# Differential attention: the second score pass widened to 128 rows, transposes kept in one PSUM bank and interleaved with the value product

## The reference, cut to what matters

```python
def diff_attention(q, k, v, lam):
    def attend(qb):
        s = jnp.einsum('bqhcd,bkhcd->bhcqk', qb, k).astype(jnp.float32) * scale
        p = jax.nn.softmax(s, axis=-1)
        a = p[:, :, 0] - lam_f * p[:, :, 1]
        o = jnp.einsum('bhqk,bkhd->bqhd', a, vf)
```

## Time and profile before

| | |
|---|---|
| median of 3 runs | 3091.17 us |
| profiled execution: device time | 3091.63 us |
| its span, first to last instruction | 3089.9 us |
| mean granted TensorE clock | 0.944 |
| TensorE matmul busy | 2802.0 us (91%) |
| VectorE / ScalarE / GpSimd busy | 1243.7 / 945.5 / 464.8 us |
| attention of layer 0, first score matmul to last copy of o | 2010.1 to 2234.1 us |
| attention of layer 1, first score matmul to last value product | 2764.0 to 2965.5 us |

### The profile page before, as it was taken

The page is one execution under the profiler, slowest core; times in us unless marked ns, Lnnn a source line. Parts: engine busy times, 40 slices in busy tenths (PEclk is TensorE's granted clock), DMA queues, the critical chain, the costliest instruction groups (busy, mean ns, idle before and its releaser), DMA issues. The chain is left out here.

```text
span 3089.9 us, 35833 instructions
## 1 busy us (share of the span) xinstructions
PE 2802.0 (91%) x14783; PEld 2349.1 (76%) x14783; DVE 1243.7 (40%) x1549; ACT 945.5 (31%) x1482; POOL 464.8 (15%) x277
## 2 busy tenths in 40 slices
PE   4999677999979999999947999999987999989989
PEld 1877565898768888888837999777777998767767
DVE  4742752434353333333365222255544412226652
ACT  3312332444141122111122212256522222135640
POOL 0100121332000000000001000066510000007630
PEclk9999889999989999999978999989988999989989
DMA  5531001001111111111112132221022113232112
GB/s 212 177 123 47 14 8 49 13 1 69 41 41 48 48 48 48 48 48 48 48 56 78 45 76 59 72 52 47 1 83 96 57 51 70 52 79 49 42 69 82
DMA packets 63598, 184.97 MB, mean 60 GB/s; under 512 B 7392, under 2 KB 26208, under 8 KB 61792
## 3 DMA queue, kind: packets, MB, share of 16 engines
q1 hardware_dynamic: 63456, 182.96, 18.8%
HBM read 148.93 MB, written 16.97 MB: 54 GB/s over the span
## 5 line engine op out<-in xcount | busy, mean ns | idle before, releaser
L1543 DVE TENSOR_REDUCE da_negmax<-ps 128x1 f32<-128x1040 f32 x136 | 168.8, 1241 | 118.6 <-PE ps L1421 93.6
L2030 DVE SCALAR_TENSOR_TENSOR res<-ps,gates,res 128x1024 f32<-128x1024 f32 x64 | 79.2, 1280 | 226.1 <-PE ps L2079 226.1
L1452 PE MATMUL ps<-da_aT,v 128*128 128x128 f32 (+1 forms) x1224 | 165.7, 281 | 2.5 <-DVE da_aT L1479 2.3
L1452 PEld LDWEIGHTS ps<-da_aT,v 128*128 128x128 f32 x1224 | 151.5, 196 | 19.8 <-issue 15.6
L1529 POOL TENSOR_TENSOR da_E<-da_E,da_F 128x1040 f32<-128x1040 f32 x68 | 163.3, 2401 | 5.7
L2079 PE MATMUL ps<-ff_h_lo,ff_wh 128*128 128x512 f32 x512 | 157.8, 389 | 0.0
L2079 PE MATMUL ps<-ff_h_hi,ff_wh 128*128 128x512 f32 x512 | 157.8, 389 | 0.0
L2079 PE MATMUL ps<-ff_h_hi,ff_wl 128*128 128x512 f32 x512 | 157.6, 389 | 0.0
L1993 ACT ACTIVATE ff_wh<-ff_raw 128x1024 fp32r<-128x1024 f32 x64 | 67.5, 1057 | 284.2 <-PE ps L2079 278.4
L1527 POOL TENSOR_SCALAR da_F<-da_F,da_mixed 128x1040 f32<-128x1040 f32 x68 | 77.4, 1138 | 498.9 <-DVE da_mixed L1554 497.5
L2067 PE MATMUL ps<-ffn_in_hi,ff_wh 128*128 128x512 f32 x480 | 148.8, 391 | 2.2 <-DVE ff_wl L2016 2.2
(11 more groups left out here) (426 smaller groups left out, 6308.1 us busy)
## 6 DMA issues: line engine op xcount, KB each, us to landing
ff_raw<-w_ff SPq DMA_DIRECT2D x64, 512.0 KB, 3.3
ada_w<-w_ada SPq DMA_DIRECT2D x16, 1024.0 KB, 7.3
wo_ring<-w_out SPq DMA_DIRECT2D x18, 512.0 KB, 4.8
residual_spill<-res SPq DMA_DIRECT2D x2, 4160.0 KB, 11.2
st_q<-st_q_rounded SPq DMA_DIRECT2D x32, 260.0 KB, 5.1
res<-xT SPq DMA_DIRECT2D x2, 4096.0 KB, 14.4
ada_w<-w_ada SPq DMA_DIRECT2D x4, 2048.0 KB, 26.6
pqk_raw<-w_in SPq DMA_DIRECT2D x16, 512.0 KB, 4.4
```

What stands on the lines that cost most here:

```text
L1452: mm = pe.matmul(k.ps[:, 7, 0:w], v(g // NQ, t), aT[g % 2][:, t, 0:w], start=(t == 0), stop=(t == NT - 1))
L1543: dve.tensor_reduce(nm[:, n % 4:n % 4 + 1], window(n), AX.X, ALU.max, negate=True).then_inc(s_nm, 1)
L2030: last = dve.scalar_tensor_tensor(out=res[:, m, :], in0=k.ps[:, 4 * s + 2 * t:4 * s + 2 * t + 2, :].rearrange("p c w -> p (c w)"), scalar= ...
```

## The change

It does four things.

1. The second score pass has 128 rows: stationary [q low; q low], moving the whole [k high; k low]. For this `copy` gains three DMAs of 64 x 1040 elements. Two write component 1's q low to both halves of a second tile (the slot that held the k low part); they wait for the eight earlier DMAs. The third writes component 0's q low over the other half of its own tile, and waits for those two. PIECES is 11, and `wait_built` waits for all eleven.
2. All transposes use bank 6, and bank 7 holds the value product alone. turn(i,1) now waits for the copy of batch 0, turn(i,2) for the copy of batch 1, and pv(i,0) for out(i-1).
3. On TensorE turn(i,0) moves ahead of pv(i-1,1), so that the value product stands between batches 0 and 1. On ScalarE out(i-1) moves ahead of exps(g,0) of the next iteration.
4. ScalarE's `round` moves from groups 0 and 1 of a head to groups 3 and 4, and GpSimd's `rest` from ahead of groups 1 and 2 to ahead of groups 4 and 5.

```diff
-    bank = (6, 7, 6)
+    bank = 6
...
                     elif b == 1:
-                        if g:
-                            pe.wait_ge(s_o, g)
+                        pe.wait_ge(s_at, 2 * g + 1)
                     else:
-                        pe.wait_ge(s_at, 2 * g + 1)
+                        pe.wait_ge(s_at1, g + 1)
...
                     if part == 0:
-                        pe.wait_ge(s_at1, g + 1)
-                        pe.wait_ge(s_at, 2 * g + 1)
+                        if g:
+                            pe.wait_ge(s_o, g)
...
                     if g < NG:
                         scores(g, 0)
+                    if 0 <= i < NG:
+                        turn(i, 0)
                     if i >= 1:
                         pv(i - 1, 1)
                     if 0 <= i < NG:
-                        turn(i, 0)
                         turn(i, 1)
...
-                for g in range(NG + LAG):
+                for g in range(NG + LAG + 1):
                     i = g - LAG
-                    if i >= 0:
+                    if 0 <= i < NG:
                         evacuate(act, i, 0, s_at)
+                    if i >= 1:
+                        out(i - 1)
                     if g < NG:
                         exps(g, 0)
-                        if g // NQ + 1 < heads and g % NQ < 2:
-                            stacks.round(act, g // NQ + 1, g % NQ)
+                        if g // NQ + 1 < heads and 3 <= g % NQ <= 4:
+                            stacks.round(act, g // NQ + 1, g % NQ - 3)
...
-                    if i >= 0:
-                        out(i)
...
-                    if g // NQ + 1 < heads and 1 <= g % NQ <= 2:
-                        stacks.rest(pool, g // NQ + 1, g % NQ - 1)
+                    if g // NQ + 1 < heads and 4 <= g % NQ <= 5:
+                        stacks.rest(pool, g // NQ + 1, g % NQ - 4)
...
-    PIECES = 8
+    PIECES = 11
...
         sp.wait_ge(self.s_low, done + 2)
+        sp.wait_ge(self.s_built, 16 * (before + 8))
+        for r in range(2):
+            sp.dma_start(low[half[r], :].bitcast(F32), qlow[half[1], :].bitcast(F32)).then_inc(self.s_built, 16)
+        sp.wait_ge(self.s_built, 16 * (before + 10))
+        sp.dma_start(qlow[half[1], :].bitcast(F32), qlow[half[0], :].bitcast(F32)).then_inc(self.s_built, 16)
...
-        half = slice(64 * c, 64 * c + 64)
         kk = self.k[h % 2][c]
-        return [(self.q[h % 2][c][:, qa:qa + w], kk), (self.low[half, h, qa:qa + w], kk[half, :])]
+        return [(self.q[h % 2][c][:, qa:qa + w], kk), (self.low[:, AH * c + h, qa:qa + w], kk)]
```

More of the change, by code:

```diff
@@ L1432, in turn @@
                     elif b == 1:
-                        if g:
-                            pe.wait_ge(s_o, g)
+                        pe.wait_ge(s_at, 2 * g + 1)
                     else:
-                        pe.wait_ge(s_at, 2 * g + 1)
+                        pe.wait_ge(s_at1, g + 1)
                     for j, t in enumerate(batch[b]):
-                        tr = pe.transpose(k.ps[:, bank[b], j * P:(j + 1) * P], E[g % 4][:, t * P:(t + 1) * P], k.ident[:])
+                        tr = pe.transpose(k.ps[:, bank, j * P:(j + 1) * P], E[g % 4][:, t * P:(t + 1) * P], k.ident[:])
                     tr.then_inc(s_T, 1)
@@ L1477, in evacuate @@
                 dst = aT[g % 2][:, 4 * b:4 * b + nb, 0:w]
-                src = k.ps[:, bank[b], 0:nb * P].rearrange("p (t q) -> p t q", t=nb)[:, :, 0:w]
+                src = k.ps[:, bank, 0:nb * P].rearrange("p (t q) -> p t q", t=nb)[:, :, 0:w]
                 (eng.activation(dst, src, ACT.Copy) if sem is s_at else eng.tensor_copy(dst, src)).then_inc(sem, 1)
@@ L1635, in copy @@
                 sp.dma_start(q[c][half[r], 0:L2].bitcast(F32), self.qh[half[c], :].bitcast(F32)).then_inc(self.s_built, 16)
+        qlow, before = self.low[:, h, :], self.PIECES * (h - self.head)
         sp.wait_ge(self.s_low, done + 2)
+        sp.wait_ge(self.s_built, 16 * (before + 8))
[3 more added lines that the diff above has]
+        sp.dma_start(qlow[half[1], :].bitcast(F32), qlow[half[0], :].bitcast(F32)).then_inc(self.s_built, 16)
     def wait_built(self, pe, h):
@@ L1640, in wait_built @@
             pe.wait_ge(self.s_built, 16 * self.PIECES * (h - self.head + 1))
-            pe.wait_ge(self.s_low, 2 * (h - self.head + 1))
     def passes(self, h, c, qa, w):
-        half = slice(64 * c, 64 * c + 64)
         kk = self.k[h % 2][c]
-        return [(self.q[h % 2][c][:, qa:qa + w], kk), (self.low[half, h, qa:qa + w], kk[half, :])]
+        return [(self.q[h % 2][c][:, qa:qa + w], kk), (self.low[:, AH * c + h, qa:qa + w], kk)]
 def latent_heads(nc, k, name, heads, NQ, splits, n_keys, v, scale, o_dst, e0, at0, then, then_at):
```

## The result

| | before | after |
|---|---|---|
| median, us | 3089.57 (4 runs, 3087.89 to 3092.67) | 3060.86 (4 runs, 3050.50 to 3066.28) |
| profiled execution, us | 3091.63 | 3063.95 |
| its span, us | 3089.9 | 3062.2 |
| mean granted clock | 0.944 | 0.946 |
| attention of layer 0, us | 223.8 | 196.8 |

The ratio of the times is 0.9898, with a 95% interval of 0.9874 to 0.9922: the change makes the kernel about 1.0% faster. The forecast was 3072, with a range of 3050 to 3090. The two attention rows count from the first score matmul to the last value product.

A forecast was written before the change was run, and what follows sets the result against it. TensorE was taken to set the pace. Iterations -52.1, phase ends -1.9 and -1.0, phase starts +5.0, head waits +17.9 and +3.5, clock +9.0 sum to -19.6 us from 3091.63: forecast 3072, range 3050 to 3090.

The forecast's parts named there:

- the likeliest case: Whole kernel: the forecast's own sum of terms holds and the time is 3072 us; given 60 in 100.
- the forecast's own signs of being wrong: Attention: iteration above 5.4 us, a head's first scores without a gap, or turn 1 or 2 waiting in every iteration.
- The iteration, 4.95 us: TensorE's steady attention iteration falls from 5.79 to 4.95 us; over 62 iterations -52.1 us.
- Rival 1: Score passes: gaps at pass ends stay whatever the row count; iteration 5.66 us, time 3105; one in ten.
- The waits in 4.90: Turns 1 and 2: new waits for ScalarE and VectorE fit a 4.90 us iteration by 0.06 and 0.02; 0.05 added.
- Phase starts, +5.0: Start of each attention phase: the three added DMAs delay the scores by 2.3 us in layer 0, 2.7 in layer 1.
- The chain at the heads: Later heads: late round, rest and DMAs end 25.7 us after the fifth group's start, TensorE waiting 5.9 us in layer 1.
- 17.9: Three later heads of layer 1: TensorE stands 5.9 us at each, waiting for the DMA chain, +17.9 us.
- gaps of 3.5: Later heads of layer 0: TensorE stands 1.1 to 1.2 us at each, +3.5 us.
- The clock, +9.0: Behind the three head gaps of layer 1: half clock costs 3.0 us each, +9.0 us.
- lead-in and drain as forecast: Phase ends: three iterations ahead per phase save 0.31 us each (-1.9), six at the end some 0.17 each (-1.0).
- the forecast's 0.2%, 6 us: Whole kernel: the smallest difference in time that a measurement can tell from no change, 0.2% or 6 us.

The follow-up runs named there:

- e2: The change with the second score pass back on 64 rows, without the three added DMAs: 3073.9 us, ratio 0.9936.
- e3: The kernel before with only the second score pass on 128 rows (eleven DMAs), old order, banks and places: 3060.68 us, ratio 0.9886.
- e4: The change with the norm's product on VectorE taking one tensor and two per-partition scalars instead of two tensors: 3059.12 us, ratio 0.9889.
- e5: The change with round and rest back at the head's start and the norm's product on one tensor: 3041.29 us, ratio 0.9825.
- e6: e5 with the q low copies waiting only for the four k DMAs, not all eight: 3037.66 us, ratio 0.9809.
- e7: The change with pv(i-1,1) ahead of turn(i,0) again on TensorE, all transposes still in one bank: 3099.61 us, ratio 1.0010.
- e1: The change with only the move of round and rest undone, back at the start of the head: 3047.65 us, ratio 0.9843.
- e8: The change with the q low copies waiting only for the four k DMAs, not all eight: 3051.75 us, ratio 0.9860.

## Why the prediction was right

The time came out 11 us below the 3072 forecast, inside the range, and the likeliest case happened. But two of the forecast's own signs of being wrong came in part: the first scores of the three later heads of layer 0 follow without a gap, where 1.1 us was put, and turn 2 waits in every iteration, for 0.15 us. Point by point:

1. *The iteration, 4.95 us.* Measured 4.96, scores 1.04 for 1.03. e2 and e3 show that the row count does most of it: 0.61 us under the new order, 0.75 under the old. Rival 1 is refuted. The Trainium skill's rule (TensorE: Matmul & The Clock Gate, Part 3, The mechanism), that weight loads overlap only where row groups differ, does not hold here as it stands; in e2 they stand idle for 0.25 us where the row count changes, and with the change on 128 rows throughout no such idle time is listed. (The same section also lets a load run ahead into a background weight buffer; no run here shows which buffer is used.) The forecast also read more into the rule than it says: the 64 rows of a narrow pass lie among the 128 of its neighbours, and its three loads use the same rows, so the rule gives the narrow pass no overlap either. And the earlier trace rows, on which it rested, show matmuls only, no loads.
2. *The waits in 4.90.* Turn 1 fits. Turn 2 waits 0.15 in the weight load, where 0.02 were left and 0.05 had been added.
3. *Phase starts, +5.0.* The gaps grew from 2.96 and 2.95 to 5.17 and 4.88: 2.2 for 2.3, and 1.9 for 2.7.
4. *The chain at the heads.* Forecast from the fifth group: +9.0, +18.2, +22.6, +25.7; measured +9.01, +18.03, +22.26, +25.14. TensorE was to be there at +19.8 and came at +21.93. Of these 2.1 us, 1.9 are VectorE's hold-up. **This is the step that failed**: "The head's remaining groups give TensorE 4 x 4.95" took every iteration as undisturbed, although `rest` runs in two of them. In layer 1 the error hides itself: gaps of 9.6 and hold-ups of 5.6 sum to 15.3, for 17.9. In layer 0 the hold-up alone is there, 5.6 us, for gaps of 3.5. In all 20.9 us stand against 21.4 forecast. In layer 1 the two causes had to balance, since a later TensorE waits less; that they nearly do in layer 0 is luck. (The 17.9 is also 3 x 5.9 = 17.7, rounded up.)
5. *The clock, +9.0.* Measured 5.1 behind the gaps: the term was mis-sized, since it was taken from a gap of 5.83 and the gaps were 3.2, of which one was followed by no fall at all. In e4, with gaps of 5.1 to 6.0, all three were. The clock's earlier rise in the first 27 us of both phases was not in the sum at all.

The balance of the profiled executions, 27.7 us: -1.8 ahead of attention, +2.2 start, -27.0 layer 0, -0.2 between, +1.9 start, -6.7 layer 1, +3.8 behind. The forecast had -25.7 for layer 0, and +1.1 for layer 1. With the measured terms, layer 0 should give 33 x 0.83 + 1.5 (lead-in and drain as forecast) - 5.6 = 23.2, and layer 1 29 x 0.83 + 1.5 - 9.6 - 5.6 - 5.1 = 5.3. The remainders, 3.8 and 1.4 us, have the sign and the size of the earlier rise: 0.82 instead of 0.51 over 27 us is 17 us less at the low level, 0.73 instead of 0.50 is 12, and each can give back at most half. By starts, the first five iterations take 31.3 us before and 24.3 after in layer 0, and 31.5 and 26.6 in layer 1, of which the shorter work explains 2.6 each (three iterations by 0.31 and two by 0.83); 4.4 and 2.3 are left. No experiment isolates the clock there, so this stays an argument.

**What stays open** is the clock outside the phases. e3 came out 12 us slower than its terms say, e5 and e6 some 6, and where it could be seen (behind the first phase in e3, at the start of both in e6) it lies where the clock rises after a sparse stretch. The runs of the change spread over 16 us, those of e3 over 2, those of the kernel before over 17 in the later batches, so the forecast's 0.2%, 6 us, as what a measurement can tell, was too fine. What decides when such a rise comes was not found.

## What to carry to other kernels

Keep the row count of successive matmuls the same, even where a pass on fewer rows has less to multiply: here four switches per iteration cost 0.61 us under the new order and 0.75 under the old, and filling the other 64 rows took three DMAs per head. That pass alone brought nearly the whole gain; moving the building of the operands later cost 17 us in attention. When an iteration is made shorter, price again every chain that does not shorten with it (DMAs, another engine's preparation), from the point where it starts to the point where it is wanted; and look in the trace for the longest instance of each instruction, not its median, for what was covered in the long iteration is exposed in the short one. If all users of a bank are put in a row, work must stand between them: with one bank for the transposes and the old order (e7) the whole gain was lost, while the old order with its two banks (e3) was 0.08 us per iteration behind the change.

## What was unexpected of the hardware

- A VectorE instruction on a single column with two tensor operands takes 0.22 us, or up to 2.28 if GpSimd's 128x1040 subtraction runs, and ends together with it. GpSimd's sum E + F (line 1529) holds it too where they meet, for up to 1.70 us in e1, and in e3 one product meets both and takes 2.44. With one tensor operand and two per-partition values the same product takes 0.28 in each of its 68 instances. The reciprocal beside it (0.15) and the copy from PSUM (0.68) are not held either. The Trainium skill (SBUF — State Buffer, Who interferes with whom) states the rule behind it: a VectorE instruction with two inputs in SBUF contends with a GpSimd instruction that reads SBUF, because one pair of ports is shared and works as an exclusive lock, and one with a single SBUF input does not. The traces agree (e4 for the second half), and show that even an instruction on one column is held until the other ends.
- Three nearly equal gaps of TensorE, with about the same work ahead of them, were followed by three different courses of the clock: behind 3.14 us it stayed at 1.00, behind 3.22 it fell after some 1.5 us, behind 3.25 it was at 0.50 from the first matmul on (three in 1.24 us, above). So the cost of such a gap is known to 3 us only. Behind the gaps of 5.1 to 6.0 us in e4 it was at half each time.
- Copies of 260 KB within SBUF, issued in pairs, landed in 2.9 to 3.7 us in the change, and in 4.0 to 4.8 at the layer-1 heads of e8, where four others had just been issued.
